# A hybrid encoder block on one core: the engines' queues of the attention re-ordered

## The reference

```
mod = silu(c) @ w_ada + b_ada                    # shift, scale, gate for 3 parts
x += 0.5*(1+gate0) * swiglu(mod0(rms_norm(x)))   # feed-forward 1, inner width 2816
h = mod1(rms_norm(x)); proj = h @ w_in           # q, k, v, xc, gate_b, gate_c: 512 each
q, k = rms_norm per head of 64 features, 8 heads
y_attn = softmax(q k^T / 8 + bias) v             # a chunk of 64 queries sees itself and 8 chunks before
y_conv = gate_b * causal_conv3(gate_c * xc)
y = concat(rms_norm(y_attn), rms_norm(y_conv)) @ w_out
x += (1+gate1) * y
x += 0.5*(1+gate2) * swiglu(mod2(rms_norm(x)))   # feed-forward 2
out = rms_norm(x) * g_final
```

## Time and profile before

| what | value |
|---|---|
| median of 3 runs | 1827.1 us (1824.01 to 1827.86) |
| the profiled execution's own time | 1827.81 us |
| its span in the profile | 1826.0 us |
| busy TensorE / VectorE / ScalarE / GpSimd | 1771.9 / 1163.5 / 699.8 / 499.4 us |
| mean granted TensorE clock | 0.990 |

### The profile page before, as it was taken

The page is one execution under the profiler, slowest core; times in us unless marked ns, Lnnn a source line. Parts: engine busy times, 40 slices in busy tenths (PEclk is TensorE's granted clock), DMA queues, the critical chain, the costliest instruction groups (busy, mean ns, idle before and its releaser), DMA issues.

```text
span 1826.0 us, 21464 instructions
## 1 busy us (share of the span) xinstructions
PE 1771.9 (97%) x8340; PEld 1449.4 (79%) x8340; DVE 1163.5 (64%) x1358; ACT 699.8 (38%) x899; POOL 499.4 (27%) x284
## 2 busy tenths in 40 slices
PE   6999999999999999997899998999999999999997
PEld 6888888888888888875688766888888888888886
DVE  7987766667777575454585653776454444577755
ACT  4443333333333442324444364444233332343442
POOL 1044556544100001114210241225344533310000
PEclk9999999999999999999999999999999999999998
DMA  8146654557866236221244320403332323585633
GB/s 347 41 154 217 210 172 164 201 198 250 301 212 226 90 133 206 84 80 47 81 139 149 106 69 1 158 3 110 106 131 86 98 98 102 193 320 180 235 92 116
DMA packets 86964, 269.65 MB, mean 148 GB/s; under 512 B 8288, under 2 KB 8416, under 8 KB 85344
## 3 DMA queue, kind: packets, MB, share of 16 engines
q1 hardware_dynamic: 82704, 260.94, 42.0%
q10 hardware_dynamic: 4176, 7.60, 1.1%
HBM read 215.55 MB, written 52.95 MB: 147 GB/s over the span
## 4 chain that ended last, share of the span: by engine, by line
PE 86%; issue 6%; DVE 3%; ACT 2%; POOL 1%; DMA 1%; SPq 0%; DVEq 0%; POOLq 0%; ACTq 0%
PE pair L2764 22%; PE pair L2765 22%; PE pair L2766 22%; PE pair L2758 5%; PE pair L2759 5%; PE pair L2760 5%; PE pair L3173 1%; PE pair L3195 1%; PE pair L3216 1%; PE pair L2861 0%; DVE x L1888 0%; ACT w_hi L1184 0%; DVE cb L1922 0%; POOL acc L1038 0%; DVE w_lo L1757 0%
## 5 line engine op out<-in xcount | busy, mean ns | idle before, releaser
L2764 PE MATMUL pair<-cb,w_hi 128*128 128x512 f32 x864 | 336.4, 389 | 0.8 <-DVE w_lo L1757 0.6
L2766 PE MATMUL pair<-cb,w_lo 128*128 128x512 f32 x864 | 336.1, 389 | 0.0
L2765 PE MATMUL pair<-cb,w_hi 128*128 128x512 f32 x864 | 336.1, 389 | 0.0
L2764 PE MATMUL pair<-h_hi,w_hi 128*128 128x512 f32 x824 | 322.4, 391 | 2.1 <-DVE h_lo L1894 2.1
L2765 PE MATMUL pair<-h_lo,w_hi 128*128 128x512 f32 x824 | 321.6, 390 | 0.0
L2766 PE MATMUL pair<-h_hi,w_lo 128*128 128x512 f32 x824 | 321.6, 390 | 0.0
L2764 PEld LDWEIGHTS pair<-cb,w_hi 128*128 128x128 f32 x864 | 162.2, 188 | 35.3 <-DVE w_lo L1757 1.0
L2766 PEld LDWEIGHTS pair<-cb,w_lo 128*128 128x128 f32 x864 | 162.2, 188 | 33.7
L2765 PEld LDWEIGHTS pair<-cb,w_hi 128*128 128x128 f32 x864 | 162.2, 188 | 33.6
L2764 PEld LDWEIGHTS pair<-h_hi,w_hi 128*128 128x128 f32 x824 | 155.3, 189 | 34.2 <-issue 2.1
L2766 PEld LDWEIGHTS pair<-h_hi,w_lo 128*128 128x128 f32 x824 | 155.3, 189 | 32.5
(11 more groups left out here) (285 smaller groups left out, 3200.6 us busy)
## 6 DMA issues: line engine op xcount, KB each, us to landing
raw<-hs SPq DMA_DIRECT2D x70, 512.0 KB, 3.8
ada_w<-w_ada SPq DMA_DIRECT2D x56, 512.0 KB, 4.0
raw<-w_mix SPq DMA_DIRECT2D x46, 512.0 KB, 3.6
hs<-tt SPq DMA_DIRECT2D x20, 1024.0 KB, 6.4
a<-w_f1o SPq DMA_DIRECT2D x30, 512.0 KB, 6.4
a<-w_f2o SPq DMA_DIRECT2D x30, 512.0 KB, 6.3
ga<-w_f1i SPq DMA_DIRECT2D x22, 512.0 KB, 4.4
ua<-w_f1i SPq DMA_DIRECT2D x22, 512.0 KB, 4.5
```

The costliest lines, as they stand in the source:

```text
L2764: nc.tensor.matmul(dst, lh, rh, start=first, stop=False, skip_group_check=True)
L2765: nc.tensor.matmul(dst, lh, rl, start=False, stop=False, skip_group_check=True)
L2766: return nc.tensor.matmul(dst, ll, rh, start=False, stop=False, skip_group_check=True)
```

## The change

It gives 1/sum a buffer of its own (`rexp`) and takes, expands and transposes it earlier in mixer 0; moves the convolution's statistics, scaling and casts to other steps; re-orders GpSimd's queue in mixer 0; moves mixer 0's output pieces to later rounds and changes their banks; puts two of mixer 1's output pieces into its last rounds; alternates pieces 0 and 1 of mixer 0's attention half; and moves rows of the next stage ahead in VectorE's and ScalarE's queues at each mixer's end. Amount of arithmetic and data are the same. The diff, cut:

More of the change, by code:

```diff
@@ L448, in out_chunk @@
         def out_chunk(mx, m, part):
-            return MX[mx] + MIX_CHUNKS[mx] + (OUT_CONV.index(m) if part == 0 else KD + m) // 2
+            return MX[mx] + MIX_CHUNKS[mx] + (OUT_CONV[mx].index(m) if part == 0 else KD + m) // 2
         def mod_col(sub, part, k):
@@ L474, in c_square @@
             return qsq if ct % 2 else sq
-        def c_buf(ct):
-            return qsq if ct % 2 else tmp
+        def c_buf(mx, ct):
+            return (tmp, qsq)[ct % 2] if mx else (tmp, qsq, sq, tmp)[ct]
+        C_BUFS = (3, 2)
         def h_buf(inst, m):
-            return qsq if inst == 1 and m % 2 else tmp
+            return qsq if inst in (1, 2) and m % 2 else tmp
         def rstd_count(n):
@@ L1617, in conv_part @@
                     act.wait_ge(y_tmp, KA * mx + ct + 1)
-                    nc.scalar.copy(col(y_hi, (KA + ct) * T, T), c_buf(ct)[:]).then_inc(y_hi_done, 1)
+                    nc.scalar.copy(col(y_hi, (KA + ct) * T, T), c_buf(mx, ct)[:]).then_inc(y_hi_done, 1)
                 def softmax(s):
@@ L1644, in r_expand, with r_copy @@
                     act.wait_ge(rrec_done, n + 1)
+                    rb = bass.AP(rrec[:].tensor, rrec[:].offset, [list(rrec[:].ap[0]), [1, HEADS], [0, HD]])
+                    nc.scalar.copy(rexp[mx][:].rearrange("p (h d) -> p h d", h=HEADS), rb).then_inc(y_act, 1)
+                def r_copy(qt):
+                    n = TT * mx + qt
+                    act.wait_ge(y_mm, y_step(mx, qt))
                     act.wait_ge(yacc_done, 2 * n) if n else None
[L1646 to L1651, removed]
                     nc.scalar.copy(ysq[:], bank[R_BANK][:]).then_inc(y_act, 1)
@@ L1718, in _ @@
                     act.dma_start(xs[mx, :, m * T:(m + 1) * T], xt(mx, m)).then_inc(xs_out, 16)
+                    if mx == 0 and m + 4 < KD:
+                        h_part(2, m + 4, 1)
             spread(7, col(rstd, T, T))
@@ L1802, in h_first @@
             def h_first(inst, m, sub, hf):
[L1804 to L1805 removed]
+                if inst in (1, 2):
+                    dve.wait_ge(h_ready, KD * inst + max(m - 1, 0))
                 else:
@@ L2676, in extras @@
                         conv_first(CONV_SPLIT[mx].index(s))
-                    if mx == 0 and s - 1 in OUT_FILL:
-                        x_conv(OUT_FILL.index(s - 1))
                 for s in range(AHEAD):
@@ L3014, in mixer @@
                     pe.wait_ge(xu_done, 26)
+                else:
+                    pe.wait_ge(x_done, CREDIT + 6)
                 for c in range(4):
@@ L3274, in mixer, with attn_both, out_part @@
                         mm.then_inc(h_free, 1)
-                def out_part(m, part, bk, first, last):
+                def attn_both(e):
+                    if e == 0:
+                        attn_stats()
+                    if e == KA - 1:
+                        attn_spread()
+                def out_part(m, part, bk, first, last, after=None):
                     n = out_chunk(mx, m, part)
@@ L3287, in out_part @@
                                     first and e == 0, last and e == KA - 1)
-                    mm.then_inc(w_used if m % 2 else (oc_mm, oa_mm)[part], 1)
+                        if e == KA - 1:
+                            mm.then_inc(w_used if m % 2 else (oc_mm, oa_mm)[part], 1)
+                        if after:
+                            after(e)
                 def between(s):
```

110 lines of the change are left out of this document (50 added, 60 removed).

## The result

| kernel | median, us | runs | range, us |
|---|---|---|---|
| before | 1827.5 | 4 | 1824.0 to 1830.1 |
| changed | 1797.4 | 4 | 1795.9 to 1800.7 |

The ratio is 0.9839, 95% interval 0.9817 to 0.9861: 30 us less. The profiled execution is the slowest of the four, 1800.65 us with a span of 1798.8; the forecast in its terms was 1800.0 and for the median 1799. A second set of five executions gave 1798.1 (1796.2 to 1798.6), ratio 0.9843 (0.983 to 0.9856).

What follows compares the result with a forecast made beforehand. TensorE was taken as the bound (busy 1771.9 of 1826.0 us), with only its waits and half-clock time winnable. Mixer 0's 15.4 plus mixer 1's 12.4 us off 1827.8 gave 1800.0, 1799 for the median; range 1789 to 1811.

Steps and rivals of the forecast that it cites:

- (3): Mixer 0, s=17: exponential behind a weight cast waiting for its load; GpSimd's order and later cast remove 4.8 and 0.49 us.
- (4): Mixer 0: small waits of 0.35, 0.39, 0.40, 0.25 and 0.42 us go through moved and alternated output pieces.
- (a): Mixer 0: first 1/sum stands on VectorE before the copies of s=4 and waits for exponential 7; new 2.0 us wait.
- (b): Mixer 0: the norm's power follows GpSimd's first weight half, so the spread waits 0.75 us.
- (c): Mixer 0: second 1/sum waits for exponential 15, behind chunk 2's cast at s=10 with its late load; 1.65 us.
- (d): Mixer 0: two output pieces leave s=17 and 19; the bare rounds wait 1.5 us for both.
- (e): Mixer 1's start: its first banks, now 4 to 7, wait for x pieces up to 5; 0.5 us.
- The clock in mixer 0: Mixer 0's attention: of 7.1 us lost to half clock, 2.5 us stay and 4.6 are won.
- R1: Rival, both mixers: the clock doesn't come back, 4.6 and 3.4 us not won; 1807 us, chance 0.12.
- R2: Rival, mixer 0: waits change places, (a) paid four times, (b) to (d) doubled; 10 us less won, 1809, chance 0.10.
- R3: Rival, slower: 28 VectorE operations pay for the port shared with GpSimd, 36 us at 1.3 each; 1836 us, chance 0.03.
- R4: Rival: the rounds are bound elsewhere and a new wait takes each one's place; no change, chance 0.03.

Runs made afterwards that it cites:

- recip_behind: The changed kernel with mixer 0's reciprocal (1/sum) taken behind the two copies of its round instead of ahead of them: 1793.85 us.
- gpsimd_back: The changed kernel with GpSimd's old order at mixer 0's start, the cast of chunk 3 staying at s=14: 1804.82 us.
- both_half: The changed kernel with mixer 0's reciprocal behind the copies, mixer 1's first weight casts later, and GpSimd's half 6 of mixer 0 waiting for four low parts: 1794.76 us.
- halves_later: The changed kernel with GpSimd's weight halves 5 and 6 of mixer 0 waiting for two of the attention's low parts: 1799.44 us.
- after_again: The changed kernel itself, unaltered, measured again in a second set: 1798.13 us.

## Why the prediction was right, step by step

The time was 1.6 us under the forecast, and each large term was tested by itself: mixer 1's casts made alone 11 us; undone, GpSimd's order 6.7, the place of 1/sum 5.3, the early pieces 1.4 (not clear of the scatter). With the statistics' 2.65 us and the 1.8 us of small waits, taken from the trace and not tested, that is 28.9 of 30 us. That the parts add up so well is partly luck: two of them were measured between sets, and all but the waits hold a clock that differs from execution to execution. Not tested by themselves are the later rounds of the output pieces in mixer 0, their banks, and the rows of the next stage moved ahead.

- **(1), (2), (3), (4), what goes in mixer 0:** right. No wait at the statistics, none at the 1/sum transposes, none of 4.8 us. The waits that I listed add up to 16.95 us, not quite the 17.25 that I put down. In (3) I gave GpSimd's order and the cast's new slot the gain in common; it is the order's.
- **(a)** 2.01 us for 2.0 at 817.9 for 817.4: right in cause and size.
- **(b)** 0 us in the profiled execution, 0.99 us in the second, for 0.75.
- **(c)** 1.46 for 1.65, but only in part by the cause that I named: no load is late there. Of what held up the copy, recip_behind took away 0.70 us with the reciprocal's place; 0.76 us stay behind the exponential. In gpsimd_back a cast does wait 0.96 us for its load there, and this wait is 2.52 us.
- **(d)** 0.53 + 0.70 = 1.23 for 1.5. **(e)** 0 for 0.5; in both_half, where TensorE comes there a microsecond sooner, it is 1.32 us, in halves_later 0.82.
- **Not foreseen:** 1.09 us before the attention half of mixer 0's output. I had looked at this port, put 2 us of it "inside the slacks" and excluded waits at this place only by that; behind the gains there was no slack. Idle won in mixer 0: 11.5 us for 10.85.
- **The clock in mixer 0** is the term that was mis-sized in the profiled execution: one drop of 5.0 us in place of 2.5 us. I had said that 0.8 or less over 4 us would show me wrong, and it did occur. Behind that wait the clock took 5.0 us in one trace, about 1.7 in two and nothing in four, 1.2 us on average; I did not have its size. In the profiled execution mixer 0 gave 11.5 + (7.1 - 5.0) = 13.6 us for 15.4 and mixer 1, by idle time and clock, 9.85 + 3.4 = 13.25 for 12.4. That its total still lay within 1 us of 1800.0 is two misses of opposite sign, so luck; the 1.6 us by which the median lies under the forecast go with executions of a higher clock.
- **Mixer 1:** 8.68 us for 8.67 at the casts; the pieces fill what they should; the clock back in the last two stretches. The new wait is 0.45 us for 1.3: by the same sum VectorE's queue gained 4.6 us and not the 3.8 that I followed.
- **Rivals.** R1 is not what happened: the clock came back in each stretch whose waits went, and fell, in some executions, behind the one long wait left and at mixer 1's start. R2 fell: one row tile of four pays (a), one (c). R3 named a true mechanism at a thirtieth of its size (1.09 us for 36). R4 fell.

## What to carry to other kernels

When a queue is written by hand, put an instruction that waits for a slow partner behind the ones whose operands are already there, even if its result is wanted early: moving one reciprocal behind two copies was worth 4.3 us. Trace a stall through loads to the queue that frees their slot; here GpSimd's order and not the cast's slot was worth 6.7 us. Where a pair of engines contends, delaying one side moves the collision to the next instruction; count what follows before you shift it, and compare variants that differ by 1 or 2 us only side by side.

## What the runs showed of the hardware that was not expected

The same wait of 2.01 us was followed by 10 us at the lower clock level in one execution, some 3 us in two (after_again and gpsimd_back) and none in four kernels (1.00 in each), with TensorE busy after it each time. In this kernel such a wait is to be priced at its own length and a chance of up to 5.0 us more, 1.2 us on average over the seven traces. And a long drop hides another wait: with 10 us at the lower level the norm's spread waits for nothing, in after_again with 3 us 0.99 us and in the four kernels with none 0.98 or 0.99 us.
